# Projection of q, k and v as three products of rounded parts, in a two-layer diffusion step on one core

## The reference

```
h  = rmsnorm(x, norm1_g) * (1 + scale) + shift          # scale, shift from SiLU(cond) @ w_mod + b_mod
q, k, v = split(h @ attn_wqkv, 3)                       # 8 heads, q and k as two halves of 64, v of 128
q, k    = axial_rope(q, k)                              # latent tokens only
p = softmax(q_half k_half^T / 8)                        # two maps per head, over latent and cached keys
o = (p[0] - lam * p[1]) @ v
y = rmsnorm(o) * (1 - lam_init) @ attn_wo
```

## Time and profile before

| | us |
|---|---|
| median of 3 runs | 3680.73 (3679.54 to 3680.92) |
| the profiled execution | 3688.61 |
| its span, first to last instruction | 3686.8 |
| PE busy in the span | 3348.8 (91%) |
| DVE busy | 1480.3 (40%) |
| ACT busy | 807.6 (22%) |
| POOL busy | 629.1 (17%) |

### The profile page before, as it was taken

How to read it: one execution, slowest core, us unless ns; L and a number is a source line. 1 busy time by engine, 2 the same in 40 slices (tenths; PEclk the granted TensorE clock), 3 DMA queues, 4 the chain that set the end, 5 groups by cost and what they waited for, 6 DMA issues and landing times. The chain is left out here.

```text
span 3686.8 us, 57439 instructions
## 1 busy us (share of the span) xinstructions
PE 3348.8 (91%) x23344; PEld 2949.3 (80%) x23344; DVE 1480.3 (40%) x2471; ACT 807.6 (22%) x1794; POOL 629.1 (17%) x526
## 2 busy tenths in 40 slices
PE   7999999997893999999999997274999999999995
PEld 3666666765453999999999997164999999999995
DVE  2455555553356333333333332865333333333332
ACT  2555555565110001001011011220010010110111
POOL 1333333443110000001001001530000010010011
PEclk9999999997895999999999999586999999999997
DMA  5222222122235877877877872156778778778783
GB/s 194 76 77 77 77 75 73 59 67 95 89 113 197 281 261 253 293 257 262 289 251 272 288 242 96 50 197 228 258 253 292 257 263 290 249 272 290 240 276 115
DMA packets 408715, 722.85 MB, mean 196 GB/s; under 512 B 15985, under 2 KB 319762, under 8 KB 408626
## 3 DMA queue, kind: packets, MB, share of 16 engines
q1 hardware_dynamic: 397010, 682.75, 53.5%
q0 software_dynamic: 11616, 38.94, 4.1%
HBM read 673.40 MB, written 48.23 MB: 196 GB/s over the span
## 5 line engine op out<-in xcount | busy, mean ns | idle before, releaser
L1328 PE MATMUL bank<-ex_xT,ring 128*128 128x144 f32 x11264 | 1391.1, 287 | 5.6 <-DVE ex_xT L1404 5.6
L1328 PEld LDWEIGHTS bank<-ex_xT,ring 128*128 128x128 f32 x11264 | 1387.5, 191 | 6.4 <-issue 5.8
L1345 PE MATMUL bank<-ex_hid,ring 128*128 128x144 f32 x5632 | 698.5, 287 | 0.0
L1345 PEld LDWEIGHTS bank<-ex_hid,ring 128*128 128x128 f32 x5632 | 691.6, 190 | 0.9
L538 POOL TENSOR_TENSOR acc<-acc,prod 128x1280 f32<-128x1280 f32 x112 | 321.1, 2889 | 560.7 <-ACT prod L731 560.7
L554 PE MATMUL bank<-wh,hT 128*128 128x384 f32 x1152 | 391.4, 494 | 0.0
L1368 ACT ACTIVATE ex_ge<-bank 128x432 f32<-128x432 f32 (+1 forms) x128 | 64.0, 500 | 1307.7 <-PE bank L1328 1307.7
L1284 POOL DMA_INDIRECT xres_lat<-ex_ye,ex_si x32 | 51.9, 1623 | 1748.3 <-ACT ex_ye L1382 1748.3
L554 PEld LDWEIGHTS bank<-wh,hT 128*128 128x128 f32 x1152 | 214.2, 191 | 165.8 <-issue 32.0
L1418 DVE RECIPROCAL ex_t<-ex_t 128x432 f32<-128x432 f32 (+1 forms) x128 | 336.4, 2628 | 4.5
L1417 DVE TENSOR_SCALAR ex_t<-ex_ge 128x432 f32<-128x432 f32 (+1 forms) x128 | 46.9, 366 | 664.4 <-ACT ex_ge L1368 664.4
(11 more groups left out here) (197 smaller groups left out, 2443.6 us busy)
## 6 DMA issues: line engine op xcount, KB each, us to landing
ring<-in_expert_w_gate SPq DMA_DIRECT2D x96, 1536.0 KB, 8.7
ring<-in_expert_w_up SPq DMA_DIRECT2D x96, 1536.0 KB, 12.3
ring<-in_expert_w_down SPq DMA_DIRECT2D x96, 1536.0 KB, 12.4
ring<-in_expert_w_gate SPq DMA_DIRECT2D x32, 1024.0 KB, 6.1
ring<-in_expert_w_up SPq DMA_DIRECT2D x32, 1024.0 KB, 8.6
ring<-in_expert_w_down SPq DMA_DIRECT2D x32, 1024.0 KB, 18.3
wmr<-in_w_mod SPq DMA_DIRECT2D x64, 384.0 KB, 3.7
wmr<-in_w_mod SPq DMA_DIRECT2D x64, 256.0 KB, 3.1
```

The costliest lines, as they stand in the source:

```text
L1328: last = nc.tensor.matmul(bank[:, banks[j % 2], f * CAP:(f + 1) * CAP], wv[:, c, f * P:(f + 1) * P], xT[:, c], start=(c == 0), stop=(c == ...
L1345: last = nc.tensor.matmul(bank[:, YB[m // 3], (m % 3) * CAP:(m % 3 + 1) * CAP], wv[:, q, m * P:(m + 1) * P], hid[:, f], start=(f == 0), st ...
```

## The change

- **Split projection.** The hidden state and the projection weights are kept as a rounded part and a remainder, both of the type `float32r`: `hTh` and `hTl`, `whh` and `whl`. A tile's projection is three products per chunk of 128 rows, high by high, high by low and low by high, in place of one float32 product.
- **Set-up.** VectorE evicts all 24 pieces to a ring of four buffers `hfull`; ScalarE copies each into `hTh`; VectorE (even pieces) and GpSimd (odd ones) subtract to get `hTl`. The two lambda sums move in between. `wm` now lies under `hTh` and `hTl`.
- **Weights.** Weights arrive in `wraw`; ScalarE copies them into `whh` (`high`) and VectorE writes the remainder over them (`low`), a quarter of a head at a time: head 0 before the first tile, head 1 during the first nine tiles, head `h + 2` in steps 2 to 5 of head `h`.
- **Buffers.** One `qT` in place of two, rotary tables of 64 columns in place of 128, `ot` of two tiles in place of two heads.
- **SP's queue.** Every head output tile is stored by itself, one store per step. The first piece of `w_mod` of the next head is loaded in the last step of a head, `wo` in step 1 of head 7.

```diff
-        hT, wh_at = sb("hT", [P, DC, N_TOK], persistent_end)
-        wh, wh_end = sb("wh", [P, 2, DC, 3 * VD], wh_at)
+        hTh, wh_at = sb("hTh", [P, DC, N_TOK], persistent_end, F32R)
+        hTl, wh_at = sb("hTl", [P, DC, N_TOK], wh_at, F32R)
+        whl, wh_end = sb("whl", [P, 2, DC, 3 * VD], wh_at, F32R)
+        wraw, _ = sb("wraw", [P, 2, DC, 3 * VD], wh_at)
+        whh, wh_end = sb("whh", [P, 2, DC, 3 * VD], wh_end, F32R)
...
-                wm, off = sb("wm", [P, NT, DC, BANK], off)
+                wm, _ = sb("wm", [P, NT, DC, BANK], persistent_end)
...
+                def low_part(eng, ops, n):
+
+                    t0, nt = ((0, 4), (4, 4), (8, 1))[n // DC]
+                    c = n % DC
+                    eng.wait_ge(hi_ok, n + 1)
+                    cols = slice(t0 * P, (t0 + nt) * P)
+                    ops.tensor_tensor(hTl[:, c, cols], hfull[:, n % 4, 0:nt * P], hTh[:, c, cols].bitcast(F32),
+                                      ALU.subtract).then_inc(lo_ok[n % 2], 1)
...
+                    def high_part(n):
+
+                        t0, nt = ((0, 4), (4, 4), (8, 1))[n // DC]
+                        act.wait_ge(hT_ok, n + 1)
+                        nc.scalar.activation(hTh[:, n % DC, t0 * P:(t0 + nt) * P], hfull[:, n % 4, 0:nt * P], ACT.Copy
+                                             ).then_inc(hi_ok, 1)
...
+                    for n in range(1, 3 * DC, 2):
+                        low_part(pool, nc.gpsimd, n)
...
+                        for c in range(DC):
+                            dve.wait_ge(xT_mm, n + 1)
+                            if n >= 4:
+                                dve.wait_ge(lo_ok[n % 2], (n - 4) // 2 + 1)
+                            nc.vector.tensor_scalar(hfull[:, n % 4, 0:nt * P], bank[:, n % 8, 0:nt * P],
+                                                    gains[:, 0, c, cond:cond + 1],
+                                                    modc[:, SHIFT1 * DC + c, cond:cond + 1], ALU.mult, ALU.add
+                                                    ).then_inc(hT_ok, 1)
+                            n += 1
+                            if n >= 2 and n % 2 == 0:
+                                low_part(dve, nc.vector, n - 2)
...
-                qT, off = sb("qT", [P, 2, N_TOK], off)
+                qT, off = sb("qT", [P, N_TOK], off)
...
-                ot, off = sb("ot", [P, 2, TT, VD], off)
+                ot, off = sb("ot", [P, 2, VD], off)
...
+                    def store_o(k):
+                        h, n = k // TT, k % TT
+                        sp.wait_ge(S["o_evac"], k + 1)
+                        sp.dma_start(rows(oscr, n)[:, h * VD:(h + 1) * VD], ot[:, k % 2]).then_inc(o_out[k % 2], 16)
...
+                    load_wm(0, 0)
+                    for k in range(STEPS + 1):
+                        h, n = k // TT, k % TT
+                        if k < STEPS and n + 1 < DC:
+                            load_wm(h, n + 1)
+                        if n == LAST and h + 1 < H:
+                            load_wm(h + 1, 0)
+                        if k < STEPS and n == 1:
+                            if h + 2 < H:
+                                sp.wait_ge(S["qkv_mm"], TT * (h + 1))
+                                load_qkv_weights(sp, h + 2)
+                            if h:
+                                store_kv(h)
+                                if h + 1 < H:
+                                    load_cache(h + 1)
+                        if k == STEPS - LT:
+                            sp.wait_ge(S["qkv_mm"], STEPS)
+                            sp.dma_start(wo[:], a["attn_wo"][0].rearrange("(h p) d -> p h d", p=P)).then_inc(wo_in, 16)
+                        if k:
+                            store_o(k - 1)
...
-                            last = nc.tensor.matmul(bank[:, qkv_bank(g), 0:3 * VD], hT[:, c, t * P:(t + 1) * P], wh[:, h % 2, c],
-                                                    start=(c == 0), stop=(c == DC - 1))
+                            if t == 0 and c % 2 == 0:
+                                pe.wait_ge(w_lo[h % 2], 4 * (h // 2) + c // 2 + 1)
+                            for i, (x, w) in enumerate(((hTh, whh), (hTh, whl), (hTl, whh))):
+                                last = nc.tensor.matmul(bank[:, qkv_bank(g), 0:3 * VD], x[:, c, t * P:(t + 1) * P], w[:, h % 2, c],
+                                                        start=(c == 0 and i == 0), stop=(c == DC - 1 and i == 2))
...
+                    def high(h, i):
+
+                        act.wait_ge(w_in[h % 2], 48 * (h // 2 + 1))
+                        if h >= 2:
+                            act.wait_ge(S["qkv_mm"], TT * (h - 1))
+                        nc.scalar.activation(whh[:, h % 2, 2 * i:2 * i + 2], wraw[:, h % 2, 2 * i:2 * i + 2], ACT.Copy
+                                             ).then_inc(w_hi[h % 2], 1)
...
                         if k + TT < STEPS:
                             values(k + TT)
+                        if 2 <= n < 6 and k < STEPS and h + 2 < H:
+                            high(h + 2, n - 2)
...
+                    def low(h, i):
+
+                        dve.wait_ge(w_hi[h % 2], 4 * (h // 2) + i + 1)
+                        nc.vector.tensor_tensor(whl[:, h % 2, 2 * i:2 * i + 2], wraw[:, h % 2, 2 * i:2 * i + 2],
+                                                whh[:, h % 2, 2 * i:2 * i + 2].bitcast(F32), ALU.subtract).then_inc(w_lo[h % 2], 1)
...
                             rotate(k + TT)
+                        if 2 <= n < 6 and h + 2 < H:
+                            low(h + 2, n - 2)
```

More of the change, by code:

```diff
@@ L8 @@
 F32 = mybir.dt.float32
+F32R = mybir.dt.float32r
 U32 = mybir.dt.uint32
@@ L288, in _ @@
                         normalise(t)
-                    act.wait_ge(gains_ok, 2)
-                    for n in range(1, 3 * DC, 2):
-                        hT_out(n)
+                    for n in range(DC):
+                        high_part(n)
                     act.wait_ge(ssq_ok, TT + 1)
                     nc.scalar.activation(lsum[:, 2:4], lsum[:, 0:2], ACT.Exp).then_inc(lam_ok, 1)
+                    for n in range(DC, 3 * DC):
+                        high_part(n)
                 @block.gpsimd
@@ L353, in _ @@
                                                        1.0, colsA[:, 96:96 + DC], ALU.add, ALU.mult
[L354 to L368, removed]
+                                                       ).then_inc(mod_ok, 1)
@@ new lines, in _ @@
+                    dve.wait_ge(mod_ok, NT + 2)
+                    n = 0
+                    for g, (t0, nt) in enumerate(((0, 4), (4, 4), (8, 1))):
+                        if g == 1:
+                            dve.wait_ge(s_lam, 64)
+                            dve.wait_ge(ssq_ok, TT)
+                            step.link(nc.vector.tensor_tensor_reduce(sq[:, 0:HD], lrow[:, 0], lrow[:, 1], 1.0, 0.0, ALU.mult,
+                                                                     ALU.add, lsum[:, 0:1]))
+                            nc.vector.tensor_tensor_reduce(sq[:, 0:HD], lrow[:, 2], lrow[:, 3], 1.0, 0.0, ALU.mult, ALU.add,
+                                                           lsum[:, 1:2]).then_inc(ssq_ok, 1)
+                        cond = 1 if t0 == LT else 0
+                        for c in range(DC):
[9 more added lines that the diff above has]
+                                low_part(dve, nc.vector, n - 2)
@@ L451, in attention @@
                 o_out = [sem(st, f"at_o_out{i}") for i in range(2)]
+                w_hi = [sem(st, f"at_w_hi{i}") for i in range(2)]
+                w_lo = [sem(st, f"at_w_lo{i}") for i in range(2)]
                 block = st.enter_context(nc.Block())
@@ L731, in products @@
                             nc.scalar.activation(dst, wm[:, i % 2], ACT.Copy, scale=silu[:, cond, c:c + 1]).then_inc(S["prod_ok"], 1)
+                    def high(h, i):
[4 more added lines that the diff above has]
+                                             ).then_inc(w_hi[h % 2], 1)
+                    for i in range(4):
+                        high(0, i)
                     cache_out(0)
@@ L735, in _ @@
                         values(g)
+                        if 2 <= g < 6:
+                            high(1, g - 2)
                         if g:
@@ L821, in modulation @@
                         last.then_inc(S["modc_done"], 1)
+                    def low(h, i):
+                        dve.wait_ge(w_hi[h % 2], 4 * (h // 2) + i + 1)
+                        nc.vector.tensor_tensor(whl[:, h % 2, 2 * i:2 * i + 2], wraw[:, h % 2, 2 * i:2 * i + 2],
+                                                whh[:, h % 2, 2 * i:2 * i + 2].bitcast(F32), ALU.subtract).then_inc(w_lo[h % 2], 1)
+                    for i in range(4):
+                        low(0, i)
                     dve.wait_ge(S["tab_in"], 32)
@@ L825, in _ @@
                         rotate(g)
+                        if 2 <= g < 6:
+                            low(1, g - 2)
```

74 lines of the change are left out of this document (20 added, 54 removed).

## The result

The median went from 3680.73 us (5 runs, 3679.54 to 3685.75) to 3697.24 us (5 runs, 3696.32 to 3700.38): a ratio of 1.0044, interval 1.0032 to 1.0056, slower by 16.5 us. The forecast was 3696. The profiled execution took 3699.75 us, its span 3697.9 (3686.8 before), and the granted clock fell from 0.941 to 0.936.

A forecast was written before the change was run, and what follows sets the result against it. PE's step and a ring through GpSimd, VectorE and ScalarE were taken as two bounds 0.2 us apart, only one shortened. Set-up, ring and sums outweighed the gains: +15.3 us, 3696 us on the median, range 3610 to 3712.

The forecast's parts named there:

- The ring: Attention steps: GpSimd's adds, difference, rotation, V copy, products, next adds; weight copies lengthen turns to 11.64 us, +12.2 us.
- The rounded matmul: PE's projection: 24 rounded passes, each between 128 and 329 ns, make a tile 3.96 us, 1.30 less.
- the first head: Head 0's projection, where only PE bounds: nine tiles, each shorter by 1.30 us, give -11.7 us.
- between heads: Two steps without adds: PE's 1.30 us a tile comes through in part, -0.8 us seven times, -5.6 us.
- Copies and subtractions: Weight parts in steps 2 to 5: ScalarE's copy 0.80 us; VectorE's subtraction 0.95 us, covered and costing nothing.
- Set-up: Before attention: VectorE does all 24 evictions and 12 subtractions, with nothing hiding this before the barrier: +14.4 us.
- The sums: PE's 40 sums at a head's end run at a lower clock after a wait: 1.07 us seven times, +7.5 us.
- The tables: Rotary tables before the first head, half as large and in pieces half as long: -0.5 us, ends 0 and -2.5.
- Smaller parts: Tables -0.5 us, last store -1.0; w_mod's buffer, one q buffer, rotary products and stores by tile cost nothing.
- the last store: End of attention: it carries one tile in place of nine, and the stage ends when it lands: -1.0 us.
- The rival on the faster side: Difference gets between GpSimd's two adds, so PE's 9.7 us bounds steps: 3613 us, or 3650 in part; chance 0.18.
- The third rival: PE's projection: a rounded pass costs what an fp32 pass does, 7.9 us a tile: 3884 us; chance 0.15.

The follow-up runs named there:

- run 4: Changed kernel without the product of the activations' low part with the weights' high part, two products in place of three: 3684.69 us, ratio 1.0009.
- run 3: Changed kernel with ScalarE's copy of the weights' high part moved behind its step's products, VectorE's subtraction one step later: 3684.14 us, ratio 1.0009.
- run 1: Changed kernel with VectorE's rotation of the next tile put ahead of its difference: 3631.44 us, ratio 0.9864.
- run 5: Changed kernel with GpSimd's second add of every step cut to one column: 3604.97 us, ratio 0.9798.
- run 2: Kernel before the change, with VectorE's rotation put ahead of its difference: 3681.83 us, ratio 1.0000.
- run 6: Kernel before the change, with GpSimd's second add of every step cut to one column: 3674.17 us, ratio 0.9981.
- run 7: Kernel before with one q buffer, half-width tables, outputs stored by tile and SP's new queue order, projection still fp32: 3679.86 us, ratio 0.9996.
- run 8: Changed kernel with twelve scrap matmuls on PE ahead of the sums of each of the first seven heads: 3686.73 us, ratio 1.0014.
- run 9: Changed kernel with rotation ahead of difference and every fourth set-up eviction on ScalarE in place of VectorE: 3630.98 us, ratio 0.9868.

## Why the prediction was right

The forecast was 15.3 us slower, and 16.5 were measured. The mechanism was right; that the total is so close is in part luck, since errors of both signs cancel in it. By its own steps:

- **The ring.** Right: +12.2 forecast, +12.25 measured; turns of 11.6 and 10.9 us against 11.64 and 10.84. That it is this ring and not PE is shown from both ends: taking a third of PE's projection away does not move the steps (run 4); taking the copy out of the ring (run 3) shortens the steps with a copy by 0.7 us (the copy takes 0.84), and taking the difference (run 1) or an add (run 5) out shortens them to 10.0 us, PE's own step. That the kernel before had two bounds 0.2 us apart is shown by runs 2 and 6, where the ring is opened and PE's 11.0 us remain.
- **The rounded matmul.** Cheaper than an fp32 instruction, as forecast, but less so: 174 ns at a granted clock of 1.00, where the forecast's 3.96 us a tile has 165. That figure, and with it the 1.30 us a tile in the terms of the first head (-11.7) and between heads (-5.6) and PE's step of 9.7 us, was the author's estimate between 128 and 329 ns; no run shows what it rests on. The runs show 24 x 174 ns, 4.18 us a tile, 1.08 less than fp32's 5.26, and a step of 10.0 us (runs 1 and 5). 174 is also just outside the 160 to 170 that the prediction gave as its sign. With 24 x 9 matmuls the difference is 2 us, about what the first head gave less (-9.8 for -11.7); the traces of runs 6 and 7 have 72.3 and 72.8 us in this row, those of runs 3, 5 and 8 have 62.2 to 62.7, so the match to a tenth is luck.
- **Copies and subtractions.** A copy takes 0.84 us (forecast 0.80), a subtraction of VectorE 0.96 (0.95), and it stayed covered: no step was longer than the ring.
- **Set-up.** +14.8 for +14.4, with a pair period of 2.11 us for 2.23. Shorter pairs gave 0.8 us back. Holds by GpSimd's subtractions, which the sum had at nothing and only the upper end named, took 1.5: two of VectorE's operations stood until one was over (a sum, 1.24 us in place of 0.22, and at 66.72 a subtraction of 128 columns, 0.79 us in place of 0.29). The size is read from the traces alone; the one run that meant to shorten set-up (run 9) did not.
- **The sums.** +9.0 us of busy time for +7.5, and run 8 shows their cause. Between the heads the whole change is +4.1 for a forecast of +1.9. In heads 0 to 5 both terms were taken too small. From the sums' start to the next projection (the sums, the product behind them and the scores) PE took 12.0 to 12.1 us before in five of the six, and now 13.7 in all: +1.6 us a head where I took 1.07, for the work behind the sums is slowed too, as the upper end had it. From that projection to the next adds it took 18.87 us before and now 17.82: -1.05 us a head where I took -0.8, a guess between two ends.
- **The tables.** -1.4 us to PE's first instruction where I took -0.5 of 0 to -2.5; run 7 has it with the tables and without the split.
- **Smaller parts.** Nothing, as run 7 shows. The -1.0 us of the last store does not show either: from the last adds to the end it is 2763.5 us in run 7 and 2763.4 in run 2. The 4.9 us of a store that the prediction read as its longest is a median.

The errors partly cancel. Against the trace of run 2, whose profiled execution lies at its kernel's median, measured less forecast is -0.9, -0.8, +1.2, 0.0, +2.0, +0.4 and +0.6 us in the rows of the table: +2.5 in all, as much as the profiled execution of the changed kernel lies above its own median.

**The rival on the faster side** (the prediction's second) did not come, but by little. `cneg` asks at 259.32 and the first add, 2.9 us long, ends at 259.35; the second add goes ahead, and `cneg` takes 2.94 us. It is as close in every such step, 2.87 us after the adds' start (in the next one 270.94 after 268.07), since ScalarE's products release the adds and stand just before the copy of the head output and the exponents that `cneg` waits for. The third rival (passes as slow as fp32) fell with the 174 ns.

Run 1 shows most sharply what stands for GpSimd's adds and what does not: in the same adds, the sine products, with one input from PSUM, keep their 0.48 us, and the addition after them, with two from SBUF, takes 0.79 us for 0.42 and ends 0.28 us after the adds. `cneg` waits for no semaphore of GpSimd and in the changed kernel still takes 2.94 us (259.32) where it takes 0.22 free of the adds, so these two engines do not meet only at semaphores, as the first section has it.

## What to carry to other kernels

When the engine that is busy all the time and a chain across three other engines have periods within a few per cent, price the chain too: here the faster projection alone bought nothing (ratio 1.0044), and the copy that its new operands need was paid in the chain (0.84 us a step). Look in the chain for the one instruction that waits for a resource and see whether something behind it could run meanwhile; here two lines in another order were worth 66 us, and only together with the faster projection. Where TensorE now waits, look at what it does next: here the sums after the wait ran at a granted clock of 0.57.

## What the runs showed of the hardware that was not expected

- A 128x384 matmul on rounded operands starts every 174 ns at a granted clock of 1.00 and every 320 ns at 0.50, its weight load included, against 329 ns for each of an fp32 product's two instructions at 1.00 in the kernel before.
- VectorE's second sum over 64 columns in the changed kernel's set-up took 1.24 us while GpSimd's subtraction ran (56.23 to 57.49), and the first, just before it, 0.22.
- The gaps between heads don't change smoothly with what is in them. From the sums' start to the next projection PE takes about 10.4, 12.0, 13.7 or 15.3 us and little between, in heads 0 to 5 of all traces, also from one head to the next with the same work: in the kernel before 12.06 us after head 1 and 13.68 after head 2, in run 3 15.30 after head 0 and 13.65 after head 1. It is in this stretch that the clock is low (in head 1 of the changed kernel 0.57 in the sums and 0.66 in the 5.5 us after them). It is low there without a wait, too: 0.71 in the kernel before from 310.2 to 316.5, where the sums start 0.05 us after the adds and PE was busy up to them. Why the stretch's length goes in steps of some 1.6 us stays open.
